# Gate sums of an HGRN block by a restarted scan on VectorE instead of products with segment patterns on TensorE

## What is computed

```python
b = jnp.cumsum(lfc, axis=2)                       # log gates summed within a chunk
o_inter = einsum('bhck,bhkv->bhcv', qc * exp(b), state)
decay = exp(where(causal, b[t] - b[s], -inf))     # for each pair t >= s of a chunk
attn = einsum('bhtk,bhtsk,bhsk->bhts', qc, decay, kc)
o = o_inter + einsum('bhts,bhsv->bhtv', attn, vc)
new_state = exp(b_last) * state + einsum('bhsk,bhsv->bhkv', kc * exp(b_last - b), vc)
```

## Time and profile before

| | us |
|---|---|
| median of 3 runs | 2145.88 (2145.47 to 2146.93) |
| the profiled execution, its own time | 2146.56 |
| its span, first to last instruction | 2144.8 |
| TensorE busy | 2101.6 (98%) |
| VectorE busy | 1223.3 (57%) |
| ScalarE busy | 984.5 (46%) |
| chain that ended last | PE 83%, DVE 7%, issue 5%, ACT 4% |
| mean granted clock of TensorE | 0.997 |

### The profile page before, as it was taken

The page is one execution under the profiler, slowest core; times in us unless marked ns, Lnnn a source line. Parts: engine busy times, 40 slices in busy tenths (PEclk is TensorE's granted clock), DMA queues, the critical chain, the costliest instruction groups (busy, mean ns, idle before and its releaser), DMA issues.

```text
span 2144.8 us, 34507 instructions
## 1 busy us (share of the span) xinstructions
PE 2101.6 (98%) x12165; PEld 1720.8 (80%) x12165; DVE 1223.3 (57%) x1921; ACT 984.5 (46%) x1493; POOL 9.2 (0%) x12
## 2 busy tenths in 40 slices
PE   7999999999999999999999999999999999999998
PEld 6877777778888888888878777877888888888887
DVE  7856676655665544443378666766556555444432
ACT  5677744445444323322256676355544443233223
POOL 1000000000000000000000000000000000000000
PEclk9999999999999999999999999999999999999999
DMA  6232232234333333333342322322343333333331
GB/s 173 70 80 70 70 65 74 72 87 122 100 108 99 99 95 94 97 94 99 84 130 65 80 70 68 72 74 60 99 122 99 112 95 98 93 95 98 96 94 66
DMA packets 373273, 195.12 MB, mean 91 GB/s; under 512 B 29692, under 2 KB 367464, under 8 KB 373096
## 3 DMA queue, kind: packets, MB, share of 16 engines
q1 hardware_dynamic: 368568, 185.29, 31.3%
q10 hardware_dynamic: 4528, 7.54, 1.1%
HBM read 190.70 MB, written 2.10 MB: 90 GB/s over the span
## 4 chain that ended last, share of the span: by engine, by line
PE 83%; DVE 7%; issue 5%; ACT 4%; DMA 1%; DVEq 0%; ACTq 0%; SPq 0%
PE PS L626 24%; PE PS L627 23%; PE PS L628 23%; DVE st L1638 1%; PE PS L891 1%; PE PS L930 1%; ACT wH L1049 1%; PE PS L911 1%; PE PS L707 1%; PE PS L708 1%; PE PS L706 1%; DVE wL L1444 1%; PE PS L896 1%; DVE dec L1609 0%; ACT dec L1220 0%
## 5 line engine op out<-in xcount | busy, mean ns | idle before, releaser
L1049 ACT ACTIVATE wH<-raw 128x1024 fp32r<-128x1024 f32 (+3 forms) x382 | 376.8, 988 | 831.8 <-PE PS L628 782.5
L626 PE MATMUL PS<-hH,wH 128*128 128x512 f32 x1680 | 664.3, 395 | 2.0 <-DVE ytmp L1567 2.0
L627 PE MATMUL PS<-hL,wH 128*128 128x512 f32 x1680 | 654.4, 390 | 0.0
L628 PE MATMUL PS<-hH,wL 128*128 128x512 f32 x1680 | 654.3, 389 | 0.0
L1444 DVE TENSOR_TENSOR wL<-raw,wH 128x1024 fp32r<-128x1024 f32 (+3 forms) x382 | 432.0, 1131 | 178.6 <-ACT wH L1049 177.9
L626 PEld LDWEIGHTS PS<-hH,wH 128*128 128x128 f32 x1680 | 315.4, 188 | 72.4 <-issue 3.4
L627 PEld LDWEIGHTS PS<-hL,wH 128*128 128x128 f32 x1680 | 315.5, 188 | 66.1 <-issue 2.9
L628 PEld LDWEIGHTS PS<-hH,wL 128*128 128x128 f32 x1680 | 315.4, 188 | 66.2
L1408 DVE TENSOR_TENSOR gate<-PS,rh 128x512 f32<-128x512 f32 x92 | 63.6, 691 | 183.3 <-PE PS L628 182.8
L628 PE MATMUL PS<-fH,wL 128*128 128x512 f32 x352 | 136.9, 389 | 0.0
L626 PE MATMUL PS<-fH,wH 128*128 128x512 f32 x352 | 136.9, 389 | 0.0
(11 more groups left out here) (360 smaller groups left out, 2917.1 us busy)
## 6 DMA issues: line engine op xcount, KB each, us to landing
raw<-in_w_in SPq DMA_DIRECT2D x106, 512.0 KB, 3.9
raw<-in_ffn_w_in SPq DMA_DIRECT2D x88, 512.0 KB, 3.8
raw<-in_xa_w_kv SPq DMA_DIRECT2D x32, 512.0 KB, 3.8
raw<-in_ffn_w_out SPq DMA_DIRECT2D x32, 512.0 KB, 3.6
raw<-in_w_mix_out SPq DMA_DIRECT2D x16, 512.0 KB, 3.6
raw<-in_xa_w_q SPq DMA_DIRECT2D x16, 512.0 KB, 3.6
raw<-in_xa_w_o SPq DMA_DIRECT2D x16, 512.0 KB, 3.6
raw<-in_ffn_w_out SPq DMA_DIRECT2D x16, 384.0 KB, 3.2
```

What stands on the lines that cost most here:

```text
L626: nc.tensor.matmul(o, w0, xh(k0 + k), start=(first and k == 0), stop=False)
L627: nc.tensor.matmul(o, w0, xl(k0 + k), start=False, stop=False)
L628: ins = nc.tensor.matmul(o, w1, xh(k0 + k), start=False, stop=(last and k == kts - 1))
L1049: nc.scalar.activation(weights_of(n, wH, NS), weights_of(n, raw, NR), ACT.Copy).then_inc(*did("scalar", "hi", n))
```

## The change

The sums come from VectorE. `hg_b` (new) makes one running sum of the log gates over all 512 tokens that restarts at each chunk: a scan `gsums = gsums * restart + t0`, where `restart` is 1 and at a chunk's first token 0. `SUF` is the chunk's last sum minus the running one, and a level is the difference to the sum in the middle of each pair of blocks, one instruction for the lower and one for the upper blocks; level 1 is the log gate itself. ScalarE takes seven exponentials of 128x512, in place. `hg_m` multiplies with keys and queries for the whole head, `hg_q` makes `qcum`. `f_4`, `hg_lf`, `hg_exp`, `hlf`, `lfS`, `segM`, the patterns in the table and their load are gone. `hg_attn` waits for VectorE in the first half only. The plan's order changes: `hg_out`(h, 1) comes after the next head's first `gate_c`, `hg_attn`(h, 1) ahead of the second `y_c`, and `hg_out`(h, 0) behind it; `hg_b`(0), `hg_m`(0) and `hg_q`(0) stand around `hg` 0, ahead of `gm_mix`. `attn` has a buffer for each half; some temporaries have other places in SBUF.

```diff
-HG, CH, BL = 4, 32, 64
-NCH, NBL = T // CH, T // BL
+HG, CH = 4, 32
+NCH = T // CH
...
-    p += [u("gu", 0), ("gm_mean",), u("gu", 1), ("f_1", 0), u("gu", 2), ("gm_var",), ("f_2", 0), ("angle", 1), u("gu", 3), ("f_3", 0), ("angle", 2), ("f_4", 0)]
-    p += [u("hi", 0), ("angle", 3), u("hq", 0), ("gm_vt",), ("angle", 4), u("hg", 0), ("hg_lf", 0), ("hg_vt", 0), ("sin",), ("gm_mix",)]
+    p += [u("gu", 0), ("gm_mean",), u("gu", 1), ("f_1", 0), u("gu", 2), ("gm_var",), ("f_2", 0), ("angle", 1), u("gu", 3), ("f_3", 0), ("angle", 2)]
+    p += [u("hi", 0), ("angle", 3), u("hq", 0), ("gm_vt",), ("angle", 4), ("hg_b", 0), u("hg", 0), ("hg_m", 0), ("hg_q", 0), ("hg_vt", 0), ("sin",), ("gm_mix",)]
     for h in range(HG):
         n = h + 1
         more = n < HG
         nxt = [u("hf", n), u("hq", n), u("hi", n), u("hg", n)] if more else [u("cq", 0), u("cq", 1), u("cq", 2), u("gate_b", 0)]
-        p += ([("hg_lf", h)] if h else [("hg_exp", 0, 0)]) + [u("gate_c", 2 * h)]
-        p += [("hg_exp", h, 0), u("y_c", 2 * h), ("hg_rs", h - 1), nxt[0]] if h else [nxt[0], u("y_c", 2 * h)]
+        p += [u("gate_c", 2 * h)] + ([("hg_out", h - 1, 1), ("hg_m", h), ("hg_q", h), u("y_c", 2 * h), ("hg_rs", h - 1), nxt[0]] if h else [nxt[0], u("y_c", 2 * h)])
         p += [("hg_attn", h, 0), u("gate_c", 2 * h + 1), ("hg_state", h, 0)] + ([("f_1", n)] if more else [])
-        p += ([("hg_norm", h - 1)] if h else []) + [u("y_c", 2 * h + 1), ("hg_exp", h, 1), nxt[1], ("hg_out", h, 0)] + ([("f_2", n)] if more else [])
-        p += ([("hg_ob", h - 1)] if h else [])
-        p += [("hg_attn", h, 1), nxt[2], ("hg_state", h, 1)] + ([("f_3", n), ("f_4", n)] if more else []) + [nxt[3], ("hg_out", h, 1)]
-        p += [("hg_vt", n)] if more else []
+        p += ([("hg_norm", h - 1)] if h else []) + [nxt[1], ("hg_attn", h, 1)] + ([("f_2", n)] if more else []) + [u("y_c", 2 * h + 1), ("hg_out", h, 0)]
+        p += ([("hg_ob", h - 1)] if h else []) + [nxt[2], ("hg_state", h, 1)]
+        p += [("f_3", n), nxt[3], ("hg_b", n), ("hg_vt", n)] if more else [nxt[3], ("hg_out", h, 1)]
...
-        segM = at("segM", 46, [P, (NL + 2) * BL], F32R)
...
-        hlf = at("hlf", W + 8, [P, NBL, 2, BL], F32R)
-        lfS = [at("lfS0", W + 10, [P, NBL // 2, P], F32R), at("lfS1", 47, [P, NBL // 2, P], F32R)]
+        gsums = at("gsums", 47, [P, T])
+        restart = at("restart", W + 18, [P, T])
         t0 = at("t0", W + 11, [P, T])
         t1 = at("t1", W + 12, [P, T])
         t2 = at("t2", W + 13, [P, T])
         t3 = at("t3", W + 14, [P, T])
-        dec = at("dec", W + 15, [P, NL + 2, 4, BL])
+
+        dec = [at("dec" + str(i), place, [P, T]) for i, place in enumerate((W + 15, W + 16, W + 17, 46, W + 8, W + 9, W + 10))]
 
         st = at("st", W + 19, [P, 8, P])
         suft = at("suft", W + 21, [P, 2, P])
-        attn = at("attn", W + 21.5, [P, 2, CH])
+        attn = at("attn", W + 21.5, [P, 2, 2, CH])
         mprod = at("mprod", W + 23, [P, 2, NL + 1, CH])
         onrm = at("onrm", W + 22, [P, T])
-        qcum = at("qcum", RC + 2, [P, 2, 2, P])
+        qcum = at("qcum", W + 23.75, [P, 2, 2, P])
...
-                    elif kind == "hg_lf":
-                        h = step[1]
-                        pe.wait_ge(*after(l, "lfL", h))
-                        for half in range(2):
-                            o = take(l, ("hg_lf", h, half), ("lfS", h, half))
-                            for c in range(4):
-                                ins = nc.tensor.transpose(o[:, c * P:(c + 1) * P], hlf[:, 4 * half + c].rearrange("p two t -> p (two t)").bitcast(F32), ident[:])
-                            ins.then_inc(*did("tensor", "hg_lf", h, half))
...
-                    elif kind == "hg_exp":
-
-                        h, half = step[1:]
-                        pe.wait_ge(sem("tables_in"), 16 * TABLES)
-                        if half == 0:
-                            pe.wait_ge(*after(l, "lfS", h, 1))
-                        if h == 0 and half == 0:
-                            pe.wait_ge(*after(l, "segM"))
-                        for c in range(4):
-                            o = take(l, ("hg_exp", h, half, c), ("dec", h, half, c))
-                            nc.tensor.matmul(o[:, 0:(NL + 2) * BL], lfS[half][:, c, :], segM[:], start=True, stop=True).then_inc(*did("tensor", "hg_exp", h, half, c))
                     elif kind == "hg_attn":
 
                         h, half = step[1:]
                         o = take(l, ("hg_suft", h, half), ("suft", h, half))
-                        pe.wait_ge(*after(l, "dec_k", h, half))
+                        if half == 0:
+                            pe.wait_ge(*after(l, "dec_k", h))
                         for i in range(2):
-                            ins = nc.tensor.transpose(o[:, i * P:(i + 1) * P], dec[:, SUF, 2 * i:2 * i + 2, :].rearrange("p c t -> p (c t)"), ident[:])
+                            ins = nc.tensor.transpose(o[:, i * P:(i + 1) * P], dec[SUF][:, (2 * half + i) * P:(2 * half + i + 1) * P], ident[:])
                         ins.then_inc(*did("tensor", "hg_suft", h, half))
 
-                        pe.wait_ge(*after(l, "dec_all", h, half))
+                        if half == 0:
+                            pe.wait_ge(*after(l, "dec_l", h, NL - 1))
 
                         o = take(l, ("hg_attn", h, half), ("attn_m", h, half))
                         for i in range(2):
                             for n in range(NL + 1):
                                 for c in range(4):
-                                    t0_ = (4 * i + c) * CH
-                                    tok = slice(half * T // 2 + t0_, half * T // 2 + t0_ + CH)
-                                    d = dec[:, min(n, NL - 1)].rearrange("p b t -> p (b t)")[:, t0_:t0_ + CH]
-                                    k_, q_ = (d, d) if n < NL else (hk[:, h % 2, tok], hq[:, h % 2, tok])
+                                    tok = slice(half * T // 2 + (4 * i + c) * CH, half * T // 2 + (4 * i + c + 1) * CH)
+
+                                    k_ = dec[n][:, tok] if n < NL - 1 else hk[:, h % 2, tok]
+                                    q_ = dec[n][:, tok] if n < NL else hq[:, h % 2, tok]
...
-                        ready = [("st", h, half), ("attn", h, half)]
+                        ready = [("st", h, half), ("attn", h, half), ("dec_all", h)]
...
-                act.dma_start(seg[:], a["consts"][:, C_SEG:C_SEG + (NL + 2) * BL]).then_inc(sem("seg_in"), 16)
...
-                    elif kind == "hg_lf":
-                        h = step[1]
-                        for half in range(2):
-                            act.wait_ge(*after(l, "hg_lf", h, half))
-                            nc.scalar.activation(lfS[half][:].rearrange("p c k -> p (c k)"), bank("hg_lf", h, half), ACT.Copy)\
-                                .then_inc(*did("scalar", "lfS", h, half))
-                    elif kind == "f_4":
-                        h = step[1]
-                        act.wait_ge(*after(l, "lf", h))
-                        if h:
-                            act.wait_ge(*after(l, "hg_lf", h - 1, 1))
-                        nc.scalar.activation(hlf[:, :, 0, :], t0[:].rearrange("p (c t) -> p c t", t=BL), ACT.Copy).then_inc(*did("scalar", "lfH", h))
-                    elif kind == "hg_exp":
-                        h, half = step[1:]
-                        for c in range(4):
-                            act.wait_ge(*after(l, "hg_exp", h, half, c))
-                            nc.scalar.activation(dec[:, :, c, :], bank("hg_exp", h, half, c)[:, 0:(NL + 2) * BL].rearrange("p (n t) -> p n t", t=BL), ACT.Exp)\
-                                .then_inc(*did("scalar", "dec", h, half, c))
+                    elif kind == "hg_b":
+                        h = step[1]
+                        for n in (SUF, 0, 1, 2, 3):
+                            act.wait_ge(*after(l, "sums", h, n))
+                            nc.scalar.activation(dec[n][:], dec[n][:], ACT.Exp).then_inc(*did("scalar", "dec", h, n))
+                        for n, src in ((NL - 1, t0), (CUM, gsums)):
+                            nc.scalar.activation(dec[n][:], src[:], ACT.Exp).then_inc(*did("scalar", "dec", h, n))
...
-                        dve.wait_ge(sem("seg_in"), l * 16 + 16)
-                        V.tensor_copy(segM[:], seg[:]).then_inc(*did("vector", "segM"))
+                        pass
...
-                    elif kind == "f_4":
-                        h = step[1]
-                        low(l, hlf[:, :, 1, :], t0[:].rearrange("p (c t) -> p c t", t=BL), hlf[:, :, 0, :], ("lfH", h), "lfL", h)
-                    elif kind == "hg_exp":
-                        h, half = step[1:]
-                        dve.wait_ge(*after(l, "dec", h, half, 3))
-                        dve.wait_ge(*after(l, "hk", h))
-                        V.tensor_copy(eb[:, half, :], dec[:, CUM].rearrange("p b (c t) -> p (b c) t", t=CH)[:, :, CH - 1]).then_inc(*did("vector", "eb", h, half))
```

(61 more changed lines are left out.)

18 lines of the change are left out of this document (5 added, 13 removed).

## The result

| | before | after |
|---|---|---|
| median of the runs, us | 2146.07 (2145.47 to 2146.93, 4 runs) | 2124.83 (2124.36 to 2125.46, 4 runs) |
| profiled execution, us (span) | 2146.56 (2144.8) | 2125.46 (2123.7) |
| mean granted TensorE clock of the span | 0.997 | 0.994 |

The ratio is 0.9901 with a 95% interval of 0.9884 to 0.9918: the change takes 21.2 us off. Forecast were 2122.6 us; the time came out 2.2 us above that, inside the range.

What follows compares the result with a forecast made beforehand. TensorE's stream of products was taken as the bound. Terms -19.5 - 12.8 - 4.0 - 2.0 + 2.5 + 10.7 + 1.8 = -23.3 us took the profiled 2146.56 to 2123.3, forecast as a median of 2122.6 us; range 2112 to 2136.

Steps and rivals of the forecast that it cites:

- The blocks of TensorE, -19.5: TensorE, all heads: gate transposes (0.80 us a head) and segment products (0.82 a half) go, 19.5 us less.
- The waits for `st`, `hlf`, `ytmp`, -12.8, and the latency beyond them, -4.0: TensorE's waits at the removed blocks and first gate unit go, 12.8 us; about 0.22 unrecorded for each of 18 waits, 4.
- the block entries: TensorE: fp32 blocks now lie apart, seven more a layer, 0.18 us each to enter and leave, +2.5 us.
- The second half's `suft`, -2.0: `hg_state`, second half, heads 1 and 2 of both layers: the wait of 0.51 us goes, 2.0 us in all.
- The first half's `suft` kept, 0.92 each, and 0.9 more in head 0, +1.8: `hg_state`, first half: the 0.92 us wait stays; in head 0 `suft` comes 0.9 us late, +1.8 us in all.
- The stall at `y_c` 0, +10.7: Head 0: VectorE delivers `gcL` late, so TensorE stalls 5.35 us a layer, 10.7 us in all.
- rival 1: Head 0: VectorE has more hidden slack, so the stall at `y_c` 0 is absent or short; 2112 us, chance 0.12.
- The clock: Rival at `y_c` 0: TensorE's granted clock falls in the stall for some 6 us, half lost each layer; 2129, chance 0.10.
- The costs on VectorE: VectorE: scan 1.15 us, half differences 0.37 each; +3.2 us a head, 26 in all, on an engine with 900 free.
- The cover of 0.9 us at `hg_attn`: Heads 1 to 3: the last level is ready 0.9 us before `hg_attn`; only VectorE costs beyond that fall on TensorE.
- Rival 4: VectorE bounds the heads: scan 3.35 us, half differences 0.69, 4.8 more a head, all on TensorE; 2161 us, chance 0.05.
- Rival 3: The removed waits come back at `hg_attn` and `hg_state`, since VectorE makes a head's products first; 2141 us, chance 0.11.

Runs made afterwards that it cites:

- e13: e11 plus VectorE and ScalarE serving `hg_attn`(h,0) ahead of the next head's `hf` (or `cq` 0) in heads 1 to 3; 2108.47 us, ratio 0.9822.
- e10: The changed kernel with TensorE's removed transposes and segment products put back as useless work nobody reads; 2139.69 us, ratio 0.9969.
- e5: The kernel before, its gate products and transposes kept, in an order like the changed kernel's but with the second `hg_state` one unit later; 2164.82 us, ratio 1.0088.
- e2: The changed kernel with 11, 5 and 5 useless products ahead of the waits for the first three parts of `gcL` at `y_c` 0; 2123.37 us, ratio 0.9894.
- e8: The changed kernel with head 0 reordered: both gate units and `hq` ahead of `y_c` 0, `hf` behind `hg_attn`(0,0); 2115.91 us, ratio 0.9859.
- e6: The changed kernel with the next head's gate unit `hf` ahead of `y_c` in heads 1 to 3; 2126.98 us, ratio 0.991.
- e3: The changed kernel with each scan done twice, 1.25 us more of VectorE per head; 2134.42 us, ratio 0.995.
- e11: e8 with `y_c` 1 and `hi` changed over in head 0; 2111.17 us, ratio 0.9841.
- e1: The changed kernel with, in head 0 alone, `gate_c` 1 ahead of `y_c` 0 and `hg_state`(0,0) after `hq`; 2126.7 us, ratio 0.9908.

## Why the prediction was right, and where not

The sum said -23.3 us; the two profiled executions differ by 21.1 and the medians by 21.2. Step by step:

- **The blocks of TensorE, -19.5.** Right: 128 instructions fewer (8 x 8 and 16 x 4), no transposes of gates. The busy time fell by 17.5, short by 2, since other products ran at half clock. In `e13`, whose clock stays up, it falls by 24.1; the 4.6 us beyond 19.5 are not accounted for. By their own time they are the largest term; `e10` does not separate them from the waits.
- **The waits for `st`, `hlf`, `ytmp`, -12.8, and the latency beyond them, -4.0.** None of the three is in the waits of after. The 0.22 us of latency a wait, worked out from one hole, were not measured by themselves. The period of heads 1 and 2 tests the sum: by the forecast 2.44 (blocks), 0.74 (`hlf`), 1.03 (`st`) and 0.73 (second `suft`) go, 0.3 comes for the block entries, 4.6 us; measured 4.6. The `suft` that stayed took 0.25 us a head more than the forecast kept, so the other terms gave that much more than it said. Why the waits for `st` went isn't shown: `e5` was to say and did not.
- **The second half's `suft`, -2.0.** Right: no wait there.
- **The first half's `suft` kept, 0.92 each, and 0.9 more in head 0, +1.8.** The kept one measured 1.17 in head 1, 4.7 for four where 3.7 was kept: +1.0. Head 0 has none at all: TensorE was later than I had it, by its clock, so ScalarE was in time; `e2`, with the clock up, brings 0.47 of it back. The order of the chain was right (VectorE scales `hf` at 17.7 after `gate_c`; I had 17.4), the price was small by 0.25.
- **The stall at `y_c` 0, +10.7.** The mechanism and the place were right; the size was not. `gm_mix` was to start at 107.6 and did at 107.33; the last `gcL` was to come at 115.9 and came at 115.69. `y_c` 0 was to be through at 116.6, 5.35 us late, and was at 117.69, 6.9 late, because its products ran at half clock. (The step `gm_mix` has 12 instructions on VectorE and not the 14 of rival 1; its 8.4 us are right.)
- **The clock.** This is the step that failed. I gave its fall 0.10 as a case beside the forecast (2129); it came in both layers, and it is what the forecast lacks. At full clock `y_c` 0 would end 0.7 us after the last `gcL`, at 116.4, so 1.3 us a layer are the clock's there, and 0.7 more at `hg_attn`: 4.0 in all. I had guessed 3 us a layer by a fall of 6 us; it was 2. Of these 4.0 only 1.5 can be had by a steady clock alone (`e2`), because `suft` stands behind. Single waits of up to 1.7 us in the kernel before were no ground for leaving it out: here two waits were enough, of 2.7 and 1.1 us, and elsewhere one of 1.8 (`e8`) or 1.45 us (`e6`).
- **The costs on VectorE.** The scan measured 1219 ns, I took 1.15; a half difference 419 ns by its record, with the next starting 0.34 after it, I took 0.37; VectorE 1251 us busy, forecast 1249. The groups by line:

```profile
L1571 DVE TENSOR_TENSOR dec<-gsums 128x256 f32<-128x256 f32 x32 | 13.4, 419 | 0.0
L1572 DVE TENSOR_TENSOR dec<-gsums 128x256 f32<-128x256 f32 x32 | 13.4, 419 | 0.0
L1563 DVE TENSOR_TENSOR_SCAN gsums<-restart,t 128x512 f32<-128x512 f32 x8 | 9.8, 1219 | 0.1
```

The Trainium skill ("DVE: opcode table, instruction layouts, handler registers and perf-mode slots", Datapath and trigger behaviour) has the built-in scan at half throughput; an estimate by that was some 1.2 us, and the trace agrees: 1219 ns for a 128x512 scan, 0.69 us for a plain operation of that shape. A broadcast column as an operand and every other group as the destination cost nothing here: 419 ns, where a plain 128x256 operation takes 0.42 us. The 1.15 us for the scan, scaled up from a reduction, is a near hit without a reason behind it.

- **The cover of 0.9 us at `hg_attn`.** Nearly right as a number, 0.7: with 1.25 us more of VectorE in each head (`e3`), `hg_attn` waits 0.55. Wrong in use: I wrote that only what goes beyond the cover falls on TensorE, while `e3` shows all of it doing so in heads 1 and 2, since `suft` behind it has no cover. Rival 4's price, one to one, was the right slope for these heads; its instruction costs were not met.
- **Rival 3** (the waits come back) did not happen; the period of 47.5 is in the forecast's 47 to 48. **Rival 1** was wrong: VectorE had no slack in head 0.

Clock +4.0, the stall at full clock 5.6 in place of 5.35 a layer +0.6, first `suft` +1.0, head 0's `suft` -1.8: +3.8, where +2.2 is measured against the profiled execution. The 1.6 between them are spread over terms that I can't separate, the 14 block entries (2.5 us) among them. That the time came out so near the forecast is in part luck: +5.6 of errors on one side stand against -3.4 on the other.

## What to carry to other kernels

Work moved off the bounding engine is paid at the moment when the other engines have none to spare, not by their average load: VectorE, with work in 59% of the span, handed an added 1.25 us on in full in heads 1 and 2 (`e3`). When one wait is filled with other work, look for who is served next by the same late engine; head 0 gave its 13.7 us only when the work put ahead asked nothing of VectorE and ScalarE (`e11`), and filling the hole alone gave none (`e1`). Steps moved by one or two units can cost nearly what the whole change gains (`e5`, 19 us): before moving one, look who takes its result and its PSUM banks next, and how many takers lie between.

## What was not expected of the hardware

The granted clock fell to 0.50 after two waits of 2.7 and 1.1 us, with TensorE having work in 3.13 and then 2.48 us of two stretches of five. It was back at 1.00 in the window from 120 to 125 us, after TensorE had been busy through the one before. The length of a wait does not say whether the clock will fall: single waits of 1.7 us (the kernel before, `st`) and of 1.1 and 2.2 us, seven microseconds apart (`e8`, first layer) left it at 1.00, while it fell behind a single one of 1.8 us in `e8`'s second layer and behind one of 1.45 us in `e6`. What tells them apart these runs don't show. Useless products in the waits kept it up and paid for themselves by 1.5 us (`e2`); useful ones there are worth 13.7 us (`e11`).
